# The first units of a two-block transformer kernel and its mLSTM heads, put in another order

## The chip, the cores and the metric

The kernel runs on one core of a Trainium2 chip. The metric is the device time of one execution in microseconds (us); below, a median of three runs. A core has a matrix engine (TensorE, PE in the profile; its weight loads are PEld), a vector engine (VectorE, DVE), a scalar engine (ScalarE, ACT), a general engine (GpSimd, POOL) and a queue engine (SyncE, SP). Each works through its own instruction list in order. An instruction waits on semaphores that others raise.

## The reference

The reference computes two transformer blocks in fp32 over 512 tokens of width 1024. Only the start of the first matters here:

```python
h = rmsnorm(x, norm_mix_g)
proj = h @ w_in                     # q_m, k_m, v_m, if_pre, o_pre, q_a, k_a, v_a, gate_pre
qk = silu(causal_depthwise_conv(concat([q_m, k_m]), conv_w, conv_b))
if_pre = if_pre + b_gate_if
ig, lf = if_pre[..., :4], log_sigmoid(if_pre[..., 4:])
hm = mlstm_cell(q_m, k_m, v_m, ig, lf)          # 4 heads of 256
hm = (hm - mean(hm)) * rsqrt(var(hm) + EPS) * mlstm_norm_g
y_a = sigmoid(o_pre) * hm
...                                 # windowed attention, merge, FFN; then a GLA + NSA block
```

`log_sigmoid` is computed as min(f, 0) - ln(1 + exp(-|f|)). The mLSTM cell is computed for all 512 tokens at once, in 128-token blocks: scores k·q, weights exp(...)·scores, numerators and divisor from weights·v.

## The kernel before

**Units.** All dense products are cut into units: one 1024 x 128 block of weights (512 KB) by the activations, 128 x 512 out. `UNITS` lists them in order: unit 0 and 1 are `qm` 0 and 1, unit 2 is `if` (the gates), unit 3 `vm` 0, units 4 and 5 `km` 0 and 1, unit 6 `vm` 1. Before the change unit 7 is `qm` 2 and unit 8 the output gate `om` 0. For accuracy a weight w is split into hi + lo (`WH`, `WL`), and so are the activations (`HH`, `HL`); each of a unit's eight k-blocks takes three matmuls (L947 to L949), so a unit takes 24.

**Who does what for a unit.** SP loads its weights into one of three `RAW` buffers (L886) when the split of three units earlier has read them. ACT makes `WH` (L1310), which also needs the unit of three earlier to be multiplied. The rest, `WL`, is made by DVE (L1576) or, for some odd units, by POOL (L2188). PE multiplies into a PSUM bank, and DVE evicts it, multiplied by the norm's factor `RB` (L1610).

**The start.** For each of eight k-blocks of x, ACT makes `HH` (L1296) and a square for the norm (L1302), DVE makes `HL` (L1561), and POOL adds the squares up (L2179) in an accumulator; the squares turn through two buffers. The norm's sum goes through PE (`fold`, L961), DVE (L1581) and POOL (a power, L2193) back to PE (`spread`, L987), and ACT copies the result to `RB` (L1318). Nothing can be evicted before `RB` is there. `lead` runs units 0 and 1 side by side, two k-blocks of each in turn, then unit 2.

**After the eviction.** A `qm` or `km` unit goes through a convolution on DVE (L1720 and three of L1724), a tanh on ACT (L1370) and a product on DVE (L1737). The gates take a chain of small 4 x 512 operations on DVE, then exp and ln on ACT (`gates_1`, L1379 and L1382), DVE again (`gates_2`, L1795 to L1804), and an exp (L1387). A `vm` unit, once evicted, is transposed on PE (L1012).

**Order.** One program is walked by each engine in turn; it fixes each engine's list. `quarter` and `unit` issue a unit's products with `flush` between, and `flush` issues the next step of each evicted unit (first tanh, then the product). `ahead(e, i)` issues the split of unit i + 2 and the load of unit i + 5. So the place of an `ahead`, an `evict` or a `flush` in the program sets its place in the lists of ACT and DVE. Here unit 1's tanh comes out of the `flush` inside unit 2, its product out of that inside unit 3; the gates' steps are issued in between.

**The heads.** After the gates' columns are turned (L1030), each head's scores (L1047), numerators (L1060) and transposes of hm (L1069) are spread over eight units' quarters by `Fill`.

Of the kernel before, what the change touches and what calls it, by code (L numbers as in the profile page):

```python
# [28 lines left out]
for _name, _n in [("ident", 128), ("big", 128), ("mean", 128), ("sel", 512), ("ba", 512), ("bc", 124),  # L29
                  ("m01", 124), ("glam", 128), ("unfold", 128), ("strip", 4),  # L30
                  ("residue", 4)]:
    CON[_name] = _at
    _at += _n
# [13 lines left out]
def unit_order():  # L47
# [27 lines left out]
    head(0, {1: ("if", 0, 0, 8)})  # L75
    for h in range(3):
        head(h + 1, {0: ("om", 2 * h, 0, 8), 3: ("om", 2 * h + 1, 0, 8)})
# [41 lines left out]
OB = 7  # L119

NSA_PARTS = [(0, (0, 1)), (3, (0,)), (3, (1,)), (2, (0,)), (2, (1,)), (1, (0, 1))]

# [40 lines left out]
class Order:  # L163
# [16 lines left out]
    def turn_bank(self, *key):  # L180
        self.hold(5 + self.turn % 2, *key)
# [7 lines left out]
    spread_max = scores = numerators = last_norm = gated = split_ya = none  # L189
# [163 lines left out]

def mlstm(e):
    lead(e, 0, "n1", False)
# [11 lines left out]
    e.store_vectors()  # L367
    e.turn_bank("columns")
    e.gate_columns()
    e.ring = [0, 1]  # L370
    at = 7
    for h in range(4):
        n = 8 if h < 3 else 11
        fill = Fill(e, range(at, at + n), 15)
        at += n
        e.turn_bank("max", h)
        e.spread_max(h)
        fill()
        for s in range(4):
            e.hold(SB[s % 3], "scores", h, s)  # L380
            e.scores(h, s)
            fill()
        for t in range(4):
            e.hold((OB, *SB)[t], "numer", h, t)
            e.numerators(h, t)
            fill()
        e.last_norm(h)
        fill(4)
        for j in range(2):
            e.turn_bank("hm", h, j)  # L390
        e.gated(h)
        fill()
        e.split_ya(h)
        fill()
        fill.drain(h == 3)
# [245 lines left out]
def build(nc, xT_d, wst_d, con_d, col_d, relb_d, oh_d, wa2_d, w1_d, w2_d, out_d, scr_d):  # L641
# [6 lines left out]
    with ExitStack() as ctx:  # L648
# [44 lines left out]
        con_in, col_in, table_in, vector_out = (signal(n, 16) for n in ("con_in", "col_in", "table_in", "vector_out"))  # L693
# [12 lines left out]
        def con(name, a=0, b=None, p0=0, p1=128):  # L706
            n = {"ident": 128, "big": 128, "mean": 128, "sel": 512, "ba": 512, "bc": 124, "m01": 124, "glam": 128,
# [28 lines left out]
        def spread_column(x, n=128):  # L736
# [5 lines left out]
        (hq0, hq1, hk0, hk1, hv0, hv1, so, xc, yc, th_, Mb, Md, E0, E1, WT, hm, yf_m, acol, ecol, stat, r0, r1, r2,  # L742
         r3) = parts(4608, 1024, 1024, 1024, 1024, 1028, 1028, 1024, 516, 512, 512, 512, 128, 512, 512, 1280, 1024, 512,
# [1666 lines left out]
```

## Time and profile before

| | |
|---|---|
| median of 3 runs | 2049.53 us (2048.44 to 2050.86) |
| profiled execution | 2049.81 us, span 2048.0 us |
| PE busy | 1971.6 us, 96% of the span |
| DVE busy | 1053.1 us, 51% |
| ACT busy | 635.0 us, 31% |
| POOL busy | 285.9 us, 14% |
| chain that ended last | PE 86%, DVE 9%, ACT 3% |
| granted TensorE clock, mean | 0.981 |

The span runs from the first instruction to the last. The chain that ended last is followed back from the end: a stretch of it on an engine is time in which nothing else could have helped. PE is nearly always busy, so what matters is the few stretches in which it stands still, and those in which the clock granted to it is half of full speed.

### The profile page before, as it was taken

To read this page: it belongs to the slowest core of one execution; us is meant where nothing else is said; L and a number is where in the kernel's file an instruction comes from. 1 tells how busy PE (TensorE), PEld (TensorE's weight loads), DVE (VectorE), ACT (ScalarE), POOL (GpSimd) and SP (SyncE) were. 2 spreads that over 40 slices of the span, in tenths; PEclk is the share of its full clock that TensorE was granted. 3 is DMA by queue.
4 is the path that set the end of the run, shared out by engine and by line. 5 is a ranking of instruction groups with operands and counts; after the bars stand their busy time and mean duration, and the time that the engine had idled before them with its cause. 6 is when DMAs were issued, how large, how long until landed. Compare 5 with 4: busy or idle time off the path is not lost.

```text
span 2048.0 us, 23700 instructions
## 1 busy us (share of the span) xinstructions
PE 1971.6 (96%) x9642; PEld 1596.9 (78%) x9642; DVE 1053.1 (51%) x1507; ACT 635.0 (31%) x1053; POOL 285.9 (14%) x190
## 2 busy tenths in 40 slices
PE   6999999999999999999998988999999999999997
PEld 5777788888888888888886777777777878888885
DVE  6666644344555644344344655546676644344344
ACT  4333322223333432222233322224344333222221
POOL 3122220011111111010021000111111131011012
PEclk9999999999999999999998899999999999999998
DMA  4222223232211323232322211221110322323322
GB/s 158 65 82 72 83 83 113 92 94 72 83 62 49 118 93 102 93 102 94 97 79 76 72 52 62 83 93 63 56 62 34 118 62 93 103 93 98 98 83 71
DMA packets 52444, 171.87 MB, mean 84 GB/s; under 512 B 5879, under 2 KB 9279, under 8 KB 52336
## 3 DMA queue, kind: packets, MB, share of 16 engines
q1 hardware_dynamic: 51616, 169.21, 25.9%
q8 instruction: 77, 1.26, 0.3%
q10 hardware_dynamic: 720, 1.15, 0.2%
q14 instruction: 31, 0.25, 0.0%
HBM read 168.12 MB, written 2.21 MB: 83 GB/s over the span
## 4 chain that ended last, share of the span: by engine, by line
PE 86%; DVE 9%; ACT 3%; issue 1%; POOL 1%; DMA 0%; DVEq 0%; POOLq 0%; ACTq 0%
PE PS L947 26%; PE PS L949 25%; PE PS L948 25%; PE PS L1245 1%; DVE WL L1576 1%; PE PS L1060 1%; PE PS L1047 1%; PE PS L1223 1%; PE PS L1267 1%; PE PS L1012 1%; PE PS L1084 1%; PE PS L1093 1%; PE PS L1107 1%; ACT WH L1310 1%; DVE AR L1610 1%
## 5 line engine op out<-in xcount | busy, mean ns | idle before, releaser
L947 PE MATMUL PS<-HH,WH 128*128 128x512 f32 x1368 | 549.3, 402 | 15.5 <-DVE WL L1576 12.2
L949 PE MATMUL PS<-HH,WL 128*128 128x512 f32 x1368 | 536.6, 392 | 0.0
L948 PE MATMUL PS<-HL,WH 128*128 128x512 f32 x1368 | 535.7, 392 | 0.0
L947 PE MATMUL PS<-AH,WH 128*128 128x512 f32 x1096 | 438.6, 400 | 11.5 <-DVE WL L1576 5.3
L1576 DVE TENSOR_TENSOR WL<-RAW,WH 128x1024 fp32r<-128x1024 f32 (+2 forms) x257 | 325.1, 1265 | 218.0 <-ACT WH L1310 216.3
L1310 ACT ACTIVATE WH<-RAW 128x1024 fp32r<-128x1024 f32 (+2 forms) x320 | 325.7, 1018 | 357.1 <-PE PS L949 357.0
L949 PE MATMUL PS<-AH,WL 128*128 128x512 f32 x1096 | 431.7, 394 | 0.0
L948 PE MATMUL PS<-AL,WH 128*128 128x512 f32 x1096 | 431.6, 394 | 0.0
L947 PEld LDWEIGHTS PS<-HH,WH 128*128 128x128 f32 x1368 | 258.8, 189 | 76.2 <-DVE WL L1576 10.9
L949 PEld LDWEIGHTS PS<-HH,WL 128*128 128x128 f32 x1368 | 258.5, 189 | 55.6
L948 PEld LDWEIGHTS PS<-HL,WH 128*128 128x128 f32 x1368 | 259.0, 189 | 53.5 <-issue 1.0
L947 PEld LDWEIGHTS PS<-AH,WH 128*128 128x128 f32 x1096 | 209.3, 191 | 59.2 <-issue 9.8
L2188 POOL TENSOR_TENSOR WL<-RAW,WH 128x1024 fp32r<-128x1024 f32 (+1 forms) x63 | 143.7, 2282 | 777.3 <-ACT WH L1310 777.3
L949 PEld LDWEIGHTS PS<-AH,WL 128*128 128x128 f32 x1096 | 208.8, 190 | 45.2
L948 PEld LDWEIGHTS PS<-AL,WH 128*128 128x128 f32 x1096 | 209.6, 191 | 42.4
L1610 DVE TENSOR_TENSOR AR<-PS,RB 128x512 f32<-128x512 f32 (+2 forms) x141 | 101.4, 719 | 212.7 <-PE PS L949 205.7
L2213 POOL TENSOR_TENSOR AR<-AR,RB 128x512 f32<-128x512 f32 x44 | 56.9, 1294 | 573.8 <-ACT AR L1348 573.8
L1348 ACT ACTIVATE AR<-AR 128x512 f32<-128x512 f32 x44 | 27.8, 632 | 159.1 <-DVE AR L1610 159.1
L2179 POOL TENSOR_TENSOR AR<-AR 128x512 f32<-128x512 f32 x36 | 48.2, 1346 | 144.0 <-ACT AR L1302 143.6
L1660 DVE TENSOR_TENSOR AR<-AR,PS 128x512 f32<-128x512 f32 x44 | 30.2, 687 | 71.1 <-PE PS L949 65.7
L1502 ACT ACTIVATE AR<-AR 128x128 f32<-128x128 f32 (+3 forms) x64 | 35.4, 554 | 93.1 <-DVE AR L2080 93.1
L1429 ACT ACTIVATE AR<-AR 128x256 f32<-128x256 f32 (+1 forms) x64 | 30.9, 485 | 87.8 <-DVE AR L1879 87.8
(241 smaller groups left out, 1432.1 us busy)
## 6 DMA issues: line engine op xcount, KB each, us to landing
RAW<-wst SPq DMA_DIRECT2D x288, 512.0 KB, 3.4
RAW<-wst SPq DMA_DIRECT2D x16, 384.0 KB, 3.0
RAW<-wst SPq DMA_DIRECT2D x16, 256.0 KB, 2.5
XT<-xT SPq DMA_DIRECT2D x3, 512.0 KB, 7.9
AR<-scr SPq DMA_DIRECT2D x16, 64.0 KB, 4.3
AR<-scr SPq DMA_DIRECT2D x8, 128.0 KB, 4.7
AR<-w SPq DMA_DIRECT2D x2, 512.0 KB, 4.1
out<-XT SPq DMA_DIRECT2D x4, 256.0 KB, 2.0
```

Of the source, the lines that this page charges most:

```text
L947: T.matmul(out, wh, XH[:, k, :], start=k == 0, stop=False)
L948: T.matmul(out, wh, XL[:, k, :], start=False, stop=False)
L949: m = T.matmul(out, wl, XH[:, k, :], start=False, stop=k == nk - 1)
L1310: t = A.activation(WH[:, i % NW, 0:n], RAW[:, i % NR, 0:n], ACT.Copy, scale=1.0)
L1429: t = A.activation(P, P, ACT.Exp, bias=ST[hp % 2][:, x, 0, b, i:i + 1], accum_out=ST[hp % 2][:, x, 1, b, i:i + 1])
L1502: t = A.activation(P, P, ACT.Exp, bias=NST[x][:, 0, hd, m:m + 1], accum_out=NST[x][:, 1, hd, m:m + 1])
L1576: t = V.tensor_tensor(WL[:, i % NW, 0:n], RAW[:, i % NR, 0:n], f(WH[:, i % NW, 0:n]), ALU.subtract)
L1610: return V.tensor_tensor(dst, src, rb, ALU.mult)
L1660: V.tensor_tensor(p, ffn_tile(name, j, 1), src, ALU.mult).then_inc(*bank_read.next(*free))
L2179: t = G.tensor_tensor(acc, acc, sums(norm, n), ALU.add)
L2188: t = G.tensor_tensor(WL[:, i % NW, 0:n], RAW[:, i % NR, 0:n], f(WH[:, i % NW, 0:n]), ALU.subtract)
L2213: t = G.tensor_tensor(ffn_tile(name, j, 1), ffn_tile(name, j, 0), RB, ALU.mult)
```

## The change

Six things, in the order of the program.

1. At the start ACT loads its function table on a dummy element before it waits for anything; it splits the weights of units 0 and 1 before the squares of those blocks; unit 1's `WL` goes from POOL to DVE, unit 2's from DVE to POOL (`lo_on_pool`). x is loaded whole before unit 2's weights.
2. The squares get eight buffers, so that none waits for POOL's additions.
3. The constants come in two transfers: the first 129 columns (identity and mean) on ACT's queue, the rest on SP's after unit 4's weights.
4. `lead_first` takes the place of `lead` for the first three units: `fold` comes after all of units 0 and 1 and a quarter of unit 2, `spread` two quarters later, and unit 4's split is issued behind `spread` instead of ahead of it.
5. `om` 0 and 1 become units 7 and 8, before the first head; the gates' columns are turned after them.
6. In each head the four scores stand together, with the transposes of the head before; the weights are made in place of the exponentials, the four numerators stand together, and the four divisors are one operation each over four columns. The matmuls are the same. The turn banks are 6 and 7 instead of 5 and 6, the fourth numerator's 5 instead of 7.

```diff
     head(0, {1: ("if", 0, 0, 8)})
+    add("om", 0)
+    add("om", 1)
     for h in range(3):
-        head(h + 1, {0: ("om", 2 * h, 0, 8), 3: ("om", 2 * h + 1, 0, 8)})
+        head(h + 1, {0: ("om", 2 * h, 0, 8), 3: ("om", 2 * h + 1, 0, 8)} if h else {})
...
+def lo_on_pool(i):
+
+    return i == 2 or (i % 2 == 1 and i > 1 and UNITS[i][0] in BUSY_DVE)
...
+def lead_first(e):
+
+    for i in range(3):
+        e.sum_bank("sum", i)
+    ahead(e, 0)
+    for k in range(0, 8, 2):
+        e.products(0, range(k, k + 2))
+        e.products(1, range(k, k + 2))
+    e.products(2, range(0, 2))
+    e.turn_bank("fold", "n1")
+    e.fold("n1")
+    ahead(e, 1)
+    e.products(2, range(2, 6))
+    e.turn_bank("spread", "n1")
+    e.spread("n1")
+    ahead(e, 2)
+    evict(e, 0)
+    flush_all(e)
+    evict(e, 1)
+    e.products(2, range(6, 8))
+
+
 def mlstm(e):
-    lead(e, 0, "n1", False)
+    lead_first(e)
     e.ones()
     quarter(e, 3, 0)
     e.gates_1()
...
     e.store_vectors()
+    unit(e, 7)
+    unit(e, 8)
     e.turn_bank("columns")
     e.gate_columns()
     e.ring = [0, 1]
-    at = 7
+    at = 9
     for h in range(4):
-        n = 8 if h < 3 else 11
-        fill = Fill(e, range(at, at + n), 15)
+        n = (6, 8, 8, 11)[h]
+        fill = Fill(e, range(at, at + n), 1)
         at += n
+        mlstm_scores(e, h)
+        fill.quarters(4)
+        e.weights(h)
+        fill.quarters(12 if h else 8)
+        for t in range(4):
+            e.hold((*SB, OB)[t], "numer", h, t)
+        e.numerators(h)
+        fill.quarters(6)
+        e.normed(h)
...
+def mlstm_scores(e, h):
+
+    if h < 4:
         e.turn_bank("max", h)
         e.spread_max(h)
...
+    if h:
+        e.turn_bank("hm", h - 1, 0)
+        e.gated(h - 1, 0)
+    if h < 4:
+        for x in range(3):
+            e.hold(SB[x], "scores", h, x)
+        e.scores(h, (0,))
+    if h:
+        e.turn_bank("hm", h - 1, 1)
+        e.gated(h - 1, 1)
+    if h < 4:
+        e.scores(h, (1, 2, 3))
+    flush(e)
+    if h:
+        e.split_ya(h - 1)
...
                     d.then_inc(*x_in[g].next("x", g))
-                    if g < 3:
+                    if g < 2:
                         s.load(g)
-                S.dma_start(C[:, :], con_d).then_inc(*con_in.next("con"))
+                s.load(2)
...
                 s.load(3)
                 s.load(4)
+                n = CON["big"]
+                S.dma_start(C[:, n:NCON], con_d[:, n:NCON]).then_inc(*con_rest_in.next("con_rest"))
...
                 A.dma_start(COL[:, :], col_d).then_inc(*col_in.next("col"))
+                A.dma_start(C[:, 0:CON["big"]], con_d[:, 0:CON["big"]]).then_inc(*con_in.next("con"))
+                act.wait_ge(*at("awake"))
+                A.activation(RC[:, 13:14], RC[:, 12:13], ACT.Copy, scale=1.0)
                 act.wait_ge(*at("col"))
-                for j in range(8):
-                    act.wait_ge(*at("x", (0, 1, 2, 2, 3, 3, 4, 4)[j]))
-                    s.scaled_hi("h1", HH, j, XT[:, j, :], col("mix_g", j))
-                    s.square("n1", j, XT[:, j, :])
-                    if j in (1, 3):
-                        s.split(j // 2)
-                act.wait_ge(*at("con"))
+                for js in ((0,), (1,), (2, 3), (4, 5, 6, 7)):
+                    for j in js:
+                        act.wait_ge(*at("x", (0, 1, 2, 2, 3, 3, 4, 4)[j]))
+                        s.scaled_hi("h1", HH, j, XT[:, j, :], col("mix_g", j))
+                    if js[0] < 2:
+                        s.split(js[0])
+                    for j in js:
+                        s.square("n1", j, XT[:, j, :])
```

Three places show how the lists move. On ACT, around the gates, before (L1310 is a unit's hi split, L1318 the copy to `RB`, L1370 the tanh of a `qm` or `km` unit, L1379 the gates' exp, L1382 their ln, L1387 their second exp):

```order
L1310 ACTIVATE WH<-RAW 128x1024 [waits unit_sum,raw_in1]
L1318 ACTIVATE RB<-PS 128x512 [waits pe_norm]
L1370 ACTIVATE AR<-AR 128x512 [waits dve_mlstm] x2
L1310 ACTIVATE WH<-RAW 128x1024 [waits unit_sum,raw_in2]
L1379 ACTIVATE AR<-AR 4x512 [waits dve_mlstm]
L1382 ACT_TABLE_LOAD
L1382 ACTIVATE AR<-AR,COL 4x512 [waits act_mlstm]
L1387 ACT_TABLE_LOAD
L1387 ACTIVATE AR<-AR 4x512 [waits dve_mlstm]
```

The same place after the change (L1375 the hi split, L1383 the copy to `RB`, L1435 the tanh, L1444 exp, L1447 ln, L1452 the second exp):

```order
L1383 ACTIVATE RB<-PS 128x512 [waits pe_norm]
L1375 ACTIVATE WH<-RAW 128x1024 [waits unit_sum,raw_in1]
L1435 ACTIVATE AR<-AR 128x512 [waits dve_mlstm]
L1375 ACTIVATE WH<-RAW 128x1024 [waits unit_sum,raw_in2]
L1444 ACTIVATE AR<-AR 4x512 [waits dve_mlstm]
L1447 ACT_TABLE_LOAD
L1447 ACTIVATE AR<-AR,COL 4x512 [waits act_mlstm]
L1435 ACT_TABLE_LOAD
L1435 ACTIVATE AR<-AR 128x512
L1452 ACTIVATE AR<-AR 4x512 [waits dve_mlstm]
```

The copy to `RB` now stands ahead of unit 4's hi split. Of the two tanh operations the second, unit 1's, has moved behind exp and ln, and the second table load stands before it.

On DVE, from unit 4's `WL` to the eviction of unit 3, after the change (L1647 is `WL`, L1681 an eviction, L1791 and L1795 the convolution, L1808 the product behind a tanh, L1859 the last step that the gates' exp waits for). Before, the list is the same in this stretch, but for a wait on ACT's ln that comes behind it:

```order
L1652 TENSOR_SCALAR RC<-PS 128x4 [waits pe_norm]
L1647 TENSOR_TENSOR WL<-RAW,WH 128x1024 [waits weight_hi,raw_in1]
L1681 TENSOR_TENSOR AR<-PS,RB 128x512 [waits act_norm,unit_sum]
...
L1859 SCALAR_TENSOR_TENSOR AR<-AR 4x512 [waits dve_mlstm]
L1861 MEMSET AR 4x512
L1808 SCALAR_TENSOR_TENSOR AR<-AR 128x512 [waits act_mlstm]
L1681 TENSOR_TENSOR AR<-PS,RB 128x512 [waits unit_sum]
```

Unit 4's `WL` stands ahead of the first eviction, and unit 1's product ahead of unit 3's eviction, in both lists; what has moved is on ACT.

## Rows read from the trace of the kernel before

**Rows 1.** Busy time by stretch: each engine's busy us, PEclk, DMA share, GB/s.
```profile
50.00:56.00 6.00, 6.00 (x17) 4.50 (x18) 4.46 (x5) 2.62 (x4) 0.00 (x0) 0.57 0.00 0
72.00:76.00 4.00, 4.00 (x14) 3.09 (x14) 0.00 (x0) 0.68 (x1) 2.37 (x1) 0.57 0.26 101
76.00:310.00 234.00, 234.00 (x1041) 187.98 (x1041) 139.67 (x273) 70.10 (x109) 46.65 (x32) 1.00 0.25 78
```

**Rows 2.** What PE waited for in 0 to 420 us: total, times, longest.
```profile
PE PS L947 <- DVE WL L1576: 10.9, 1, 10.9
PE PS L1012 <- DVE AR L1610: 6.9, 2, 5.7
PE PS L947 <- POOL WL L2188: 2.7, 1, 2.7
```

**Rows 3.** Readers of x, 0 to 60 us: ns min/median/max of one, starts.
```profile
L1296 ACT ACTIVATE HH<-XT,COL x8: 705/706/722, 5.9 to 18.7; 128x512 fp32r<-128x512 f32 x8
L1302 ACT ACTIVATE AR<-XT x8: 612/612/630, 6.5 to 19.8; 128x512 f32<-128x512 f32 x8
L1561 DVE SCALAR_TENSOR_TENSOR HL<-XT,COL,HH x8: 752/1770/2830, 6.7 to 20.3; 128x512 fp32r<-128x512 f32 x8
```

**Rows 4.** Users of the raw weights, 0 to 60 us.
```profile
L1310 ACT ACTIVATE WH<-RAW x8: 1039/1042/1061, 8.2 to 57.2; 128x1024 fp32r<-128x1024 f32 x8
L1576 DVE TENSOR_TENSOR WL<-RAW,WH x4: 1210/1360/2143, 9.3 to 57.1; 128x1024 fp32r<-128x1024 f32 x4
L2188 POOL TENSOR_TENSOR WL<-RAW,WH x4: 2403/2473/2803, 13.6 to 58.4; 128x1024 fp32r<-128x1024 f32 x4
DMA to landing us min/median/max: 3.4/4.0/7.4
```

**Rows 5.** POOL's additions, the same view of the arena tile.
```profile
L2179 POOL TENSOR_TENSOR AR<-AR x6: 1311/1548/1734, 8.4 to 19.9; 128x512 f32<-128x512 f32 x6
```

**Rows 6.** Timeline, the start and the lead: start us, us, instruction, idle before.
```profile
4.61 1.28 ACT L1296 ACT_TABLE_LOAD   x1 [4.61 <-DMA XT<-xT]
...
25.02 1.84 PE L961 MATMUL PS<-C,AR 128*128 128x1 f32 x16
...
32.30 1.05 PE L987 MATMUL PS<-C,RC 128*128 128x128 f32 x8
...
33.39 0.60 ACT L1318 ACTIVATE RB<-PS 128x512 f32<-128x512 f32 x1 [2.49 <-PE PS L987]
```

**Rows 7.** Timeline of DVE from the first eviction to unit 3's.
```profile
34.09 0.69 DVE L1610 TENSOR_TENSOR AR<-PS,RB 128x512 f32<-128x512 f32 x1 [0.95 <-ACT RB L1318]
...
44.76 2.55 DVE L1785 TENSOR_SCALAR AR<-AR,COL 4x512 f32<-4x512 f32 x1
...
48.50 0.61 DVE L1737 SCALAR_TENSOR_TENSOR AR<-AR 128x512 f32<-128x512 f32 x1
49.14 0.69 DVE L1610 TENSOR_TENSOR AR<-PS,RB 128x512 f32<-128x512 f32 x1
```

**Rows 8.** Timeline of ACT around the gates.
```profile
42.77 0.63 ACT L1370 ACTIVATE AR<-AR 128x512 f32<-128x512 f32 x1 [4.30 <-DVE AR L1774]
...
48.06 0.63 ACT L1379 ACTIVATE AR<-AR 4x512 f32<-4x512 f32 x1 [3.71 <-DVE AR L1788]
48.71 1.28 ACT L1382 ACT_TABLE_LOAD   x1
50.00 0.72 ACT L1382 ACTIVATE AR<-AR,COL 4x512 f32<-4x512 f32 x1
50.74 1.28 ACT L1387 ACT_TABLE_LOAD   x1
```

**Rows 9.** Timeline of PE at the stall before unit 3's transposes.
```profile
43.66 0.39 PE L948 MATMUL PS<-HL,WH 128*128 128x512 f32 x1
43.88 0.39 PE L949 MATMUL PS<-HH,WL 128*128 128x512 f32 x1
49.98 1.08 PE L1012 MATMUL PS<-C,AR 128*128 128x128 f32 x4 [5.71 <-DVE AR L1610]
```

## What the change was forecast to do, before its result was seen

> **What bounds the kernel now.** I read the busy time by stretch first. From 76 to 310 us, through all four heads, PE is busy for 234.00 of 234.00 us at granted clock 1.00 [rows 1]. The matmuls of this stretch are the same after the change, so it has nothing to give; it can only lose. What can move lies in the first 76 us. The list of what PE waited for gives three stalls there: 10.9 us until the first split weights, 2.7 us for POOL's `WL` of unit 1, 5.7 us at the transposes of unit 3 (L1012; the row's other wait, 1.2 us, comes at the entrance to attention, where the program is unchanged) [rows 2]. Two stretches run at half clock: in 50 to 56 us, after the long stall, and in 72 to 76 us, after the short matmuls of the gates' columns, the clock is 0.57, so they lose 6 x 0.43 = 2.6 and 4 x 0.43 = 1.7 us [rows 1].
>
> Then I asked what ends the third stall. PE has finished its matmuls at 44.3 and starts the transposes at 49.98 [rows 9]. It waits for DVE's eviction of unit 3 (49.14), and DVE has been in an unbroken chain since its first eviction at 34.09: two convolutions and the gates' small steps [rows 7]. That one began when ACT had written `RB`, at 33.39 + 0.60 = 33.99 [rows 6]. So all that happens on PE before 44 us is off the path unless it brings `RB` earlier. The end is set by: `RB`, what DVE does ahead of its first eviction, the chain to unit 3's eviction, the transposes.
>
> **When RB comes after the change.** The table load (1.28 us) now runs before x lands at 4.61 [rows 6]. ACT then makes `HH` 0 (0.71) and can split unit 0. Its weights are the second transfer in SP's list and land 3.4 to 7.4 us after their issue, median 4.0; before, ACT reached that split at 8.2, without a wait [rows 4]. I take 6.0 (bounds 5.3, when `HH` 0 is done, and 8.2). Split 1.04, DVE's rest 1.21 to 1.49 (the 2.14 is one beside POOL) [rows 4]: first matmul at 8.5 instead of 10.9.
>
> PE can't run ahead from there, since it needs `HL`. `HL` takes 0.75 us alone and 1.77 at the median [rows 3], because in this stretch a DVE operation with two SBUF inputs alternates with POOL's additions. The Trainium skill, "SBUF — State Buffer", Who interferes with whom, says that such an instruction and a GpSimd instruction that reads SBUF hold a shared port pair exclusively, the other blocked for the whole instruction; the trace agrees in the 0.75 against 1.77 us. By it the eight buffers don't help DVE, since they only let POOL queue its additions sooner. `HH` 2 is done at 6.0 + 1.04 + 0.61 + 0.71 + 1.04 + 0.61 + 0.71 = 10.7 [rows 3, 4]. Six `HL` at 1.77 end at 21.3 (at 0.75 throughout: 15.2). Behind the last one stand nine matmuls. One starts every 0.228 us: 43.66 and 43.88 are two neighbours [rows 9], and 24 take 5.46 us. So units 0 and 1 end at 21.3 + 2.0 = 23.3. Unit 2's `WL` is on POOL behind six additions; the last three can't begin before square 4 at about 16.0, 3 x 1.55 and then 2.4 to 2.8 end at 23.2 [rows 4, 5]. Both paths meet at 23.3; a later one alone would cost. The `HL` path alone could save 6 us, the POOL path can't: with additions of 1.31 it ends at 22.3. So 23.3 has little room below, 1 us, and more above.
>
> From there to `RB`: 18 matmuls of unit 2 (4.1), fold 1.8, spread 1.0, ACT 0.6 [rows 6]: 30.8. That is 3.2 us before the old 33.99.
>
> **Ahead of the first eviction.** Unit 4's hi split now stands behind the copy to `RB` on ACT, and its rest ahead of the eviction on DVE. Before, both were done while PE was still in `spread`. Now they cost 1.04 + 1.2 (alone) to 2.1 (beside POOL) [rows 4]; I take 1.2 and 0.1 of hand-over. First eviction at 33.1, against 34.09: of the 3.2 us, 1.0 is left.
>
> **The chain.** From 34.09 to the start of the gates' exp at 48.06 it is 13.97 us [rows 7, 8]. One step of it, 2.55 us for a 4 x 512 operation where the wider product beside it takes 0.61 [rows 7], was held by POOL's `WL` of unit 5. After the change unit 5's split comes earlier, beside unit 1's convolution, whose steps have SBUF inputs too: I leave the 1.9 us in (bounds: 1.9 less, or another 0.9, up to a POOL split of 2.8 [rows 4]). Exp starts at 47.1.
>
> Here the change adds a wait. Unit 1's tanh was issued before the gates and was done at 43.4 [rows 8]. Now it stands behind exp and ln, and ln uses another table. On ACT: exp to the second table load took 50.74 - 48.06 = 2.68, then the load 1.28 and the tanh 0.63 [rows 8], together 4.6: tanh is done at 51.7. Behind it on DVE wait unit 1's product, then unit 3's eviction, and PE's transposes behind that; from product to transposes it was 49.98 - 48.50 = 1.48 [rows 7, 9]. **PE resumes at 53.2 instead of 49.98: 3.2 us later.** The stall itself grows from 5.7 to some 13.5 us: PE, done with units 0 and 1 at 23.3, has 60 matmuls (13.7), fold and spread (2.8) until it arrives, at 39.8.
>
> Whether a table switch costs more than its row is the second rule weighed. Rows first: the load ends at 49.99 and ln starts at 50.00 [rows 8]. The Trainium skill, "ScalarE: Activation LUTs", What ACT_TABLE_LOAD costs, puts a drain of about 1.38 us beside the load, some 2.66 us for a switch. By it the two switches would cost 2.8 us more, and the sum would be 2054.1 us. The rows leave no room for it.
>
> **After the stall.** The gates' second half waits for ln no longer (DVE did, before, after unit 3's eviction), so nothing behind is later relative to PE. Half clock after resuming: 2.6 us in both [rows 1]; a stall is above the length that already halved the clock. Turning the columns and the max now stand together with 4.3 us of full-width fp32 scores behind them, and the third short matmul (the bias vector) is moved two units ahead of them. Of the 1.7 us lost in 72 to 76 [rows 1] I take all as regained; the other end is nothing.
>
> **The heads.** Md, divisors and norms are fewer and wider operations; DVE was busy 140 of 234 us [rows 1], and PE waits for none of it. The tight place is head 1's scores: unit 13's convolution and product must be done one unit plus about 1.5 us after its matmuls. By my count 1.3 us is to spare, and one clash with POOL (up to 2.4 us [rows 4]) would cost up to 1.1. Bounds 0 and 1.1; I take 0. The second part of the constants lands some 50 us before its first use, the first part lies beside the x transfers, bank numbers cost nothing.
>
> **The sum.** Own time of the profiled execution 2049.8 (0.3 above the median of the runs, and it is what I add to): + 3.2 - 1.7 = **2051.3 us**.
>
> **The rivals.**
> - *The second half-clock stretch stays.* For it: columns and max are still short matmuls in a row, some 1.6 us. Against: they were longer, and full-width work now stands on both sides. 2053.0 us.
> - *The tanh isn't last.* If ACT's switch were hidden, PE would resume at 33.1 + 15.9 = 49.0: - 1.0 - 1.7 gives 2047.1. For it: `RB` is earlier. Against: ACT and DVE take their lists in order, and the load stands right before that tanh. With POOL's clash gone as well, 1.9 less: 2045.2, faster.
> - *The cold start: slower.* PE gets its work in groups of 3 and 9 matmuls, as `HL` arrives. If it is granted half clock (0.43 us each, twice the pitch) until unit 2, units 0 and 1 take 48 x 0.43 = 20.6 from 8.5, to 29.1 instead of 23.3, and `RB` and everything behind move with it, since the path runs through `RB`: up to + 5.8, 2057.1. It decides the sign at 2.3 us, ten matmuls or so. Half the effect is 2054.2. The same place gives 1 to 2 us if x or unit 1's weights land late.
> - *The drain of the skill's page:* 2054.1, as above.
>
> **The numbers.** 0.2%, 4.1 us, is about what a measurement of this kernel can tell from no change: 2045.4 to 2053.6 counts as the same. Forecast 0.44 (own range 2049.5 to 2053); second stretch stays 0.22; tanh not last 0.11, of which 0.05 faster; cold start or late weights 0.20, of which 0.02 stay below the bound; drain 0.03. Faster 0.06, same 0.73, slower 0.21. Range 2046.5 to 2055.5: it leaves out the deep end of the cold start and the case of everything early.
>
> **What would show it.** Right: PE's first matmul near 8.5; `RB` near 31; the first eviction behind a `WL` of DVE at about 33; on ACT load, ln, load, tanh in one row; PE's wait at L1067 of 12 to 14 us, ended by DVE's eviction at 53. Wrong: this wait ending before 50.5 (then the table switch isn't on the path), `RB` after 33 (then the start is colder than taken), or any PE wait over 1 us between 80 and 310 us (then the heads have a price).

## The result, and the profile after

The changed kernel took 2054.1 us (median of 12 runs, 2049.74 to 2055.49), the kernel before on the same chip 2049.18 (12 runs, 2045.55 to 2051.50): a ratio of 1.0022, 95% interval 1.0013 to 1.0031. A second comparison, in the experiments below, gave 1.0016 [1.0007, 1.0025] (2054.17 against 2050.4 us). The forecast was 2051.3 with a range of 2046.5 to 2055.5. So the time lies in the range, but 2.8 us above the forecast, and just past the 2053.6 us at which the prediction began its slower case (chance 0.21). One of tanh_first's twelve runs below took 2229.59 us at a granted clock of 0.84; its ratio leaves that run out, and without it the median is 2050.38 instead of 2050.64 us.

The profiled execution took 2053.67 us, span 2051.9, against 2049.81 and 2048.0 before. Busy time by stretch first, with PEclk as the third number from the end, the answer to [rows 1]:

```profile
50.00:56.00 6.00, 3.40 (x11) 2.89 (x12) 4.82 (x6) 1.00 (x2) 0.00 (x0) 0.51 0.00 0
72.00:76.00 4.00, 4.00 (x21) 3.28 (x21) 1.04 (x2) 0.56 (x1) 2.39 (x1) 1.00 0.52 163
76.00:310.00 234.00, 233.42 (x1045) 187.73 (x1044) 138.66 (x226) 69.75 (x110) 44.15 (x24) 1.00 0.25 79
```

The second half-clock stretch is gone (1.00 in 72 to 76 us), and PE is busy for 233.42 of 234 us in the heads, against 234.00. What PE waited for in 0 to 310 us, against [rows 2]:

```profile
PE PS L1067 <- DVE AR L1681: 13.2, 1, 13.2
PE PS L1002 <- DVE WL L1647: 8.2, 1, 8.2
PE PS L1002 <- DVE HL L1632: 1.0, 3, 0.4
PE PS L1107 <- DVE AR L1808: 0.6, 1, 0.6
```

The long stall is 13.2 us (forecast 13.5), the first matmul starts at 8.25 (8.5), and head 1's scores wait 0.6 us (0, bound 1.1). The readers of x and POOL's additions, against [rows 3, 5]:

```profile
L1632 DVE SCALAR_TENSOR_TENSOR HL<-XT,COL,HH x8: 744/1776/1780, 5.3 to 18.7; 128x512 fp32r<-128x512 f32 x8
L2252 POOL TENSOR_TENSOR AR<-AR x6: 1550/1558/1807, 9.6 to 18.4; 128x512 f32<-128x512 f32 x6
```

`HL` still takes 1.78 us at the median. The first eight matmuls of PE start 0.43 us apart (8.84, 9.27, 9.69 and so on to 11.40), later ones 0.23, and PE then waits for `HL`. The timeline from the fold to the first eviction, against [rows 6, 7]:

```profile
24.29 1.84 PE L1016 MATMUL PS<-C,AR 128*128 128x1 f32 x16
...
29.91 0.60 ACT L1383 ACTIVATE RB<-PS 128x512 f32<-128x512 f32 x1 [7.25 <-PE PS L1042]
30.40 1.05 ACT L1375 ACTIVATE WH<-RAW 128x1024 fp32r<-128x1024 f32 x1
31.55 1.23 DVE L1647 TENSOR_TENSOR WL<-RAW,WH 128x1024 fp32r<-128x1024 f32 x1 [5.23 <-ACT WH L1375]
32.70 0.68 DVE L1681 TENSOR_TENSOR AR<-PS,RB 128x512 f32<-128x512 f32 x1
```

`RB` is written at 30.5, 3.5 us ahead of before, and unit 4's split takes 2.1 of them back: the first eviction is at 32.70, 1.4 us ahead of before. Then the gates, against [rows 7 to 9], all engines:

```profile
46.41 0.63 ACT L1444 ACTIVATE AR<-AR 4x512 f32<-4x512 f32 x1 [8.39 <-DVE AR L1859]
46.43 0.48 DVE L1861 MEMSET AR<- 4x512 f32 x1
47.06 1.28 ACT L1447 ACT_TABLE_LOAD   x1
48.35 0.72 ACT L1447 ACTIVATE AR<-AR,COL 4x512 f32<-4x512 f32 x1
49.09 1.28 ACT L1435 ACT_TABLE_LOAD   x1
50.38 0.63 ACT L1435 ACTIVATE AR<-AR 128x512 f32<-128x512 f32 x1
51.05 0.69 DVE L1808 SCALAR_TENSOR_TENSOR AR<-AR 128x512 f32<-128x512 f32 x1 [4.13 <-ACT AR L1435]
51.77 0.69 DVE L1681 TENSOR_TENSOR AR<-PS,RB 128x512 f32<-128x512 f32 x1
52.38 0.67 DVE L1866 SCALAR_TENSOR_TENSOR AR<-AR 4x512 f32<-4x512 f32 x1
52.60 1.08 PE L1067 MATMUL PS<-C,AR 128*128 128x128 f32 x4 [13.18 <-DVE AR L1681]
```

Load, ln, load, tanh stand in one row, then product, eviction, transposes: PE resumes at 52.60 (forecast 53.2, before 49.98). Up to here all is as forecast. But where the 4 us are is shown by the first transposes of the attention part (L1012 before, L1067 after), at the end of all that the change touches. Before and after:

```profile
312.01 0.63 PE L1012 MATMUL PS<-C,AR 128*128 128x128 f32 x4 [1.24 <-DVE AR L1610]
```

```profile
311.73 0.63 PE L1067 MATMUL PS<-C,AR 128*128 128x128 f32 x4 [1.24 <-DVE AR L1681]
```

The changed kernel is 0.3 us **ahead** there. It stays 0.3 to 0.4 ahead until 1092 us, and from 1202 us to the end it is 3.7 to 4.0 behind. So the loss lies in 1092 to 1200 us, the start of the GLA part, whose instructions stand in the same order in both kernels. Busy time by stretch there, before:

```profile
1116.00:1122.00 6.00, 5.01 (x23) 3.65 (x24) 2.28 (x5) 1.91 (x2) 0.00 (x0) 1.00 0.00 1
1122.00:1132.00 10.00, 10.00 (x27) 6.16 (x26) 5.55 (x9) 6.14 (x9) 0.00 (x0) 0.66 0.01 2
1142.00:1148.00 6.00, 4.65 (x21) 3.55 (x20) 3.95 (x6) 1.88 (x3) 0.00 (x0) 1.00 0.14 40
1148.00:1152.00 4.00, 4.00 (x19) 3.32 (x18) 2.61 (x4) 2.40 (x4) 0.00 (x0) 1.00 0.25 92
```

And after:

```profile
1116.00:1122.00 6.00, 4.60 (x16) 3.79 (x17) 1.54 (x3) 1.91 (x2) 0.00 (x0) 0.72 0.03 10
1122.00:1132.00 10.00, 10.00 (x41) 6.56 (x40) 6.70 (x10) 4.26 (x6) 0.00 (x0) 1.00 0.00 0
1142.00:1148.00 6.00, 1.45 (x7) 0.90 (x7) 4.06 (x7) 2.40 (x4) 0.00 (x0) 1.00 0.00 0
1148.00:1152.00 4.00, 4.00 (x11) 3.14 (x12) 2.29 (x4) 2.42 (x3) 0.00 (x0) 0.57 0.44 131
```

In the changed kernel a half-clock piece falls at 1117 to 1121 us, in the kernel before at 1123 to 1130 us. During the first, VectorE waits for what PE makes: its copy of a unit's transposes (L1768 before, L1839 after) starts at 1120.85 us before and at 1122.73 us after, and only 0.4 of these 1.9 us were there when PE took up its work at 1117 us. Before and after:

```profile
1120.85 0.69 DVE L1768 COPY AR<-PS 128x512 f32<-128x512 f32 x1 [2.45 <-PE PS L1012]
```

```profile
1122.73 0.69 DVE L1839 COPY AR<-PS 128x512 f32<-128x512 f32 x1 [3.73 <-PE PS L1067]
```

The second piece lies where PE is ahead of the engines that feed it, so the lost time comes out of a later wait. In the changed kernel PE has full clock there and arrives early: its stall for VectorE's `WL` is 4.55 us instead of 1.35, and the clock halves once more behind it (1148 to 1151 us). Going by the starts of the same VectorE operations, the changed kernel loses 0.8 us between 1092 and 1101 us (where half clock lasts 6.8 us instead of 3.4), 1.5 between 1110 and 1121, 1.6 between 1146 and 1160 and 0.3 behind that. The stall in the kernel before and in the changed one:

```profile
1146.01 0.47 PE L947 MATMUL PS<-AH,WH 128*128 128x512 f32 x1 [1.35 <-DVE WL L1576]
```

```profile
1147.88 0.58 PE L1002 MATMUL PS<-AH,WH 128*128 128x512 f32 x1 [4.55 <-DVE WL L1647]
```

### The profile page after: what moved, and what is told of

Its sections match the earlier page's. It is cut to its first block, busy times and chain, and to the rows that moved or that the text cites. A ratio compares the mean times of both kernels' runs of the same rounds, so it can differ in the third digit from the quotient of the medians.

```text
span 2051.9 us, 23633 instructions
## 1 busy us (share of the span) xinstructions
PE 1968.4 (96%) x9642; PEld 1595.8 (78%) x9642; DVE 1050.4 (51%) x1460; ACT 633.9 (31%) x1054; POOL 283.5 (14%) x182
## 4 chain that ended last, share of the span: by engine, by line
PE 85%; DVE 9%; ACT 3%; issue 1%; POOL 0%; DMA 0%; DVEq 0%; SPq 0%
PE PS L1002 25%; PE PS L1003 25%; PE PS L1004 25%; DVE WL L1647 1%; PE PS L1306 1%; PE PS L1107 1%; PE PS L1122 1%; PE PS L1284 1%; PE PS L1328 1%; PE PS L1067 1%; ACT WH L1375 1%; PE PS L1145 1%; DVE AR L1681 1%; PE PS L1154 1%; PE PS L1168 1%
## 5 line engine op out<-in xcount | busy, mean ns | idle before, releaser
L1002 PE MATMUL PS<-HH,WH 128*128 128x512 f32 x1368 | 541.7, 396 | 11.3 <-DVE WL L1647 9.5
L1375 ACT ACTIVATE WH<-RAW 128x1024 fp32r<-128x1024 f32 (+2 forms) x320 | 325.8, 1018 | 366.6 <-PE PS L1004 365.8
L1647 DVE TENSOR_TENSOR WL<-RAW,WH 128x1024 fp32r<-128x1024 f32 (+2 forms) x257 | 323.8, 1260 | 217.6 <-ACT WH L1375 215.8
L1681 DVE TENSOR_TENSOR AR<-PS,RB 128x512 f32<-128x512 f32 (+2 forms) x141 | 101.4, 719 | 235.9 <-PE PS L1004 229.8
```

What stands on the lines that cost most here:

```text
L1002: T.matmul(out, wh, XH[:, k, :], start=k == 0, stop=False)
L1375: t = A.activation(WH[:, i % NW, 0:n], RAW[:, i % NR, 0:n], ACT.Copy, scale=1.0)
L1647: t = V.tensor_tensor(WL[:, i % NW, 0:n], RAW[:, i % NR, 0:n], f(WH[:, i % NW, 0:n]), ALU.subtract)
L1681: return V.tensor_tensor(dst, src, rb, ALU.mult)
```

## The experiments

Two questions: are the 4 us fixed in the changed program (theory S), or do they hang on where half clock falls (theory C)? And do the steps of the forecast stand in the price that it gave them? "Entrance" is the start of those first transposes, "at 1202" the start of the VectorE operation that the kernel before starts at 1201.99 us; both, like "PE resumes" (after the stall), in the one profiled execution. A shift is against the first profile of before. The medians come from five comparisons; the kernel before took 2049.18 us beside changed, 2050.4 beside after_again, tanh_first, split4_first and both_first, 2048.76 beside the two `gla_filled`, stall_filled and gates_between, 2049.05 beside old_lead, three_squares and before_again, and 2049.07 beside best.

| kernel | PE resumes | entrance (shift) | at 1202, shift | profiled, us | median, us |
|---|---|---|---|---|---|
| before | 49.98 | 312.01 | 0 | 2049.81 | 2049.18 |
| before_again | 50.06 | 311.94 (-0.1) | -2.45 | 2049.37 | 2049.19 |
| changed | 52.60 | 311.73 (-0.3) | +3.72 | 2053.67 | 2054.10 |
| after_again | 52.67 | 311.61 (-0.4) | +0.20 | 2049.91 | 2054.17 |
| tanh_first | 48.73 | 308.76 (-3.2) | +0.02 | 2051.55 | 2050.64 |
| split4_first | 50.52 | 310.81 (-1.2) | -1.06 | 2050.45 | 2053.03 |
| both_first | 46.79 | 307.20 (-4.8) | -6.33 | 2043.76 | 2046.25 |
| old_lead | 46.69 | 305.66 (-6.3) | -5.70 | 2044.01 | 2046.12 |
| three_squares | 52.54 | 312.94 (+0.9) | -0.58 | 2049.49 | 2052.59 |
| gates_between | 52.68 | 313.11 (+1.1) | +5.13 | 2055.06 | 2053.84 |
| stall_filled | 52.69 | 311.90 (-0.1) | +0.13 | 2051.74 | 2052.39 |
| before_gla_filled | 50.48 | 312.14 (+0.1) | -4.06 | 2046.14 | 2047.65 |
| after_gla_filled | 52.78 | 312.05 (0.0) | -2.74 | 2047.32 | 2047.74 |
| best | 46.50 | 305.36 (-6.7) | -7.72 | 2042.31 | 2040.18 |

**after_again**: the changed kernel, unchanged.

> The changed kernel once more, to see what of its time repeats. In the first profile its mLSTM part ended 0.3 us ahead of the kernel before (transposes at the entrance to attention 311.73 against 312.01 us), and the 4 us were lost between 1101 and 1194 us, in code that both have alike. Theory C (clock): which stretches there get half clock hangs on where the chip's grants fall, so this profile has fold (L1016, 1101 us) at the same time within 0.3 us, but the stretch from there to 1194 us takes another length than 92.8 us in at least some profiles (before: 89.2). Theory S (systematic): the stretch repeats at 92.8 within 0.5 us, and the total at 2053 to 2055 us.

Its profiled execution took 2049.91 us, 3.8 less than the first one, with the same program and the same entrance. The same stretches as above:

```profile
1116.00:1122.00 6.00, 4.83 (x23) 3.63 (x24) 2.32 (x5) 1.91 (x2) 0.00 (x0) 1.00 0.01 2
1122.00:1132.00 10.00, 10.00 (x28) 6.23 (x27) 5.69 (x9) 6.00 (x9) 0.00 (x0) 0.66 0.01 2
1142.00:1148.00 6.00, 4.64 (x21) 3.55 (x20) 4.08 (x6) 1.75 (x3) 0.00 (x0) 1.00 0.12 24
```

From 1100 us on it reads as the kernel before. Theory S falls for the single execution: one program shows both courses. But the two don't come equally often. Of the 24 runs of the changed kernel 20 took over 2052 us and 4 took 2049.7 to 2050.0, with nothing between; of the 118 runs of the kernel before in the five comparisons 9 took over 2052. That the runs above 2052 are those of the long course is read from the two profiled ones (2053.67 and 2049.91 us); the others have no trace.

**before_again**: the kernel before, unchanged.

> The kernel before once more, for its trace. Theory C: up to the entrance to attention it repeats within 0.2 us (312.0), and from 1092 us on it may take another path, up to 4 us either way, with the half-clock pieces elsewhere.

Entrance within 0.1 us, the same course to 1169 us, and then a half-clock piece that the first profile has is missing, behind the same 3.7 us of idle time. First profile, then this one:

```profile
1172.00:1176.00 4.00, 2.94 (x9) 2.57 (x10) 3.97 (x6) 0.00 (x0) 0.00 (x0) 0.50 0.18 43
```

```profile
1172.00:1176.00 4.00, 3.06 (x16) 2.62 (x17) 3.84 (x6) 0.00 (x0) 0.00 (x0) 1.00 0.23 61
```

That puts it 2.45 us ahead at 1202 us; pieces elsewhere take 2.0 of it back by the end. So within the kernel before, too, half clock falls differently from one execution to the next.

**before_gla_filled** and **after_gla_filled**: the same edit in each, which gives PE full-width work in two idle times of the GLA part.

```diff
                     if k == 0:
                         s.free("sum", i)
+                        if i == unit_of("small2") + 1:
+                            for _ in range(4):
+                                T.matmul(out, ident(), con("sel"), start=True, stop=True)
                         pe.wait_ge(*at("lo", i))
...
                 if name == "small2":
+                    for _ in range(2):
+                        T.matmul(PS[:, b, :], ident(), con("sel"), start=True, stop=True)
                     pe.wait_ge(*at("tanh", i))
```

> The kernel before, with six full-width matmuls whose result is thrown away: four in the 4 us stall ahead of the GLA part's second unit (PE idle 1088 to 1092 us) and two in the 2 us wait ahead of the small gates' transposes (1115 to 1117). Nothing computed changes. Theory C (clock): the half-clock piece at 1092 to 1096 us, some 2 us of loss, goes, the pieces behind it move, and the total falls to 2045 to 2049, with less spread than the 2045.7 to 2055.0 of the kernel as it is. Theory S (a fixed cost in the program): the matmuls are hidden or cost up to 5.5 us, total 2050 or more.

> The same six thrown-away matmuls in the changed kernel. Theory C: the 4 us between the two kernels come from where the half clock falls, not from the change's own region, which ends 0.3 to 0.4 us ahead at the entrance to attention; with the same filling the two kernels' profiles should differ by under 2 us at 1200 us, and their medians by less than the 4 us they differ as they are. Theory S: the changed kernel stays 4 us above the filled kernel before.

The medians are 2047.65 (0.9989 [0.9979, 0.9998] of before) and 2047.74 us (0.9995 [0.9987, 1.0004]). The 4.9 us between the two kernels (3.8 in the second comparison) have become 0.1 by the medians and 1.2 by the ratios, whose intervals overlap, and their ranges, 2045.5 to 2049.1 and 2046.3 to 2049.9, no longer hold a group above 2052. At 1202 us the two profiles are 1.3 us apart. The filled matmuls of the kernel before and the first one behind them, then the stretch in three kernels, before, before_gla_filled, after_gla_filled (an fp32 matmul stands as two in the rows, so four are x8):

```profile
1088.13 3.59 PE L947 MATMUL PS<-C 128*128 128x512 f32 x8
1092.22 0.50 PE L950 MATMUL PS<-AH,WH 128*128 128x512 f32 x1 [0.50 <-DVE WL L1581]
```

```profile
1084.00:1098.00 14.00, 8.79 (x31) 6.51 (x30) 8.60 (x9) 5.91 (x9) 3.96 (x4) 0.88 0.29 90
```

```profile
1084.00:1098.00 14.00, 12.24 (x46) 8.18 (x45) 8.61 (x9) 6.01 (x9) 4.04 (x4) 1.00 0.27 90
```

```profile
1084.00:1098.00 14.00, 12.28 (x46) 8.25 (x45) 8.60 (x9) 5.85 (x9) 3.87 (x4) 1.00 0.28 90
```

The filled work displaces none of the real (PE takes up unit `small2` + 1 at 1092.22 in both the kernel before and the filled one), and the clock is 1.00 in this stretch. This is the experiment that shows the cause by taking it away: the half clock of 1090 to 1097 us is gone from both kernels (the changed one has none now until 1138 us), the change does not touch this part, and the difference in the median is gone with it, as far as the intervals tell.

**tanh_first**: unit 1's tanh before the gates.

```diff
     evict(e, 1)
+    flush(e)
     e.products(2, range(6, 8))
```

> Only unit 1's tanh is issued before the gates again, as it was before. My prediction's step says: the load, ln, load chain on ScalarE leaves the path. After the gates' last VectorE step at 45.7 + 0.6 come unit 1's product (0.69), unit 3's eviction (0.69) and the transposes: PE resumes at 47.8 instead of 52.6, 4.8 us earlier, and the attention entrance moves from 311.7 to about 307. Theory L (local): the total falls by as much, to about 2049. Theory C (clock): the entrance moves by 4.8, but the total by 4.8 plus or minus up to 4, as the stretch 1085 to 1194 us falls out otherwise. Rival (the tanh isn't what PE waited for): PE resumes at 52 or later, total 2054.

PE resumes at 48.73 us, 3.9 us earlier, not 4.8.

With the tanh moved, ScalarE's split of unit 5 comes behind it, POOL's `WL` of unit 5 begins at 43.24 instead of 38.16, and it lies beside a 4 x 512 operation of the gates, which takes 2.55 us instead of 0.47; in the changed kernel it lay beside unit 1's first convolution step (2.38 instead of 0.55). So the clash of [rows 7] only changes its victim, as the forecast left it in; and a memset of 0.5 us ahead of the product was forgotten in the 4.8. That the tanh is on the path of what PE waits for last is shown. Of the 3.2 us by which the entrance is ahead of the kernel before, none are left at 1202 us.

**split4_first**: unit 4's split where it was.

```diff
+    ahead(e, 2)
     e.turn_bank("spread", "n1")
     e.spread("n1")
-    ahead(e, 2)
     evict(e, 0)
```

> Only unit 4's split is moved ahead of the spread, where it was before; the tanh stays behind the gates. My prediction took 2.2 us for it: ScalarE's 1.05 and VectorE's 1.2 stand between the copy to RB and the first eviction. Expected: RB copy unchanged at 29.9, first eviction at 30.5 instead of 32.7, all of the chain 2.1 us earlier, PE resumes at 50.5 instead of 52.6, entrance to attention at 309.6. Theory L: total 2.1 lower, about 2052. Theory C: total anywhere from 2048 to 2056 with the entrance at 309.6. Rival: VectorE is held by POOL instead, and the eviction gains under 1 us.

PE resumes at 50.52, 2.1 us earlier, where the forecast's term was 2.3 (1.04 + 1.2 + 0.1). Only 0.9 of it reaches the entrance, since the half clock after the stall lasts to 56 us, as late as in the changed kernel, and the median moved by 1.1.

**both_first**: both edits.

> Both edits together: unit 4's split ahead of the spread and unit 1's tanh before the gates. If both stand in one chain, PE resumes at 45.7 instead of 52.6 (4.8 + 2.1 earlier), the stall is 6.3 us, the entrance to attention at 304.9 and by theory L the total at about 2047, below the kernel before. Theory C: entrance as said, total 2043 to 2051. Rival: something else is last once the tanh is gone (PE's own work ends at 39.4), and the sum of the two is under 5 us.

PE resumes at 46.79 (3.9 + 2.1 would be 46.6), the entrance is at 307.20 and the median 2046.25, ratio 0.9982 [0.9973, 0.9991]: below both kernels. The two terms add up in one chain.

**old_lead**: the first three units in their old order, the rest of the change kept.

```diff
 def mlstm(e):
-    lead_first(e)
+    lead(e, 0, "n1", False)
```

> The changed kernel with the order of the first three units as it was: fold ahead of the last quarter of units 0 and 1, spread after half of unit 2, units 2 to 4 split one step earlier, unit 1's tanh ahead of the gates; the rest of the change (weights ahead of squares, eight buffers, constants in two transfers, gates' move, heads) stays. From the traces: PE waits for HL in 10 to 20 us, so a fold of 1.7 us there is partly hidden, and six matmuls fewer (1.4 us) stand ahead of the spread. Expected by these rows: RB at 28.6 (30.5 in the changed kernel), PE resumes at 45 against 46.8 with both edits of the earlier run, entrance to attention at 305 to 306. Rival: the fold there waits for POOL's last addition (20.5 us) and PE loses up to 2 us, RB near 30.5 and the entrance at 307. Totals: theory C says anything from 2 below to 4 above what the entrance gives, 2041 to 2049.

Half right. `RB` comes at 30.7, not 28.6: the fold at 20.09 waited 0.6 us for POOL and took 1.92, and a half-clock piece fell behind it. The two rows are of this kernel, around the fold and after the stall:

```profile
22.00:26.00 4.00, 4.00 (x12) 3.13 (x12) 0.16 (x1) 1.06 (x1) 1.98 (x3) 0.57 0.39 131
46.00:52.00 6.00, 5.31 (x18) 3.82 (x18) 4.94 (x6) 2.71 (x3) 0.00 (x0) 0.72 0.10 39
```

PE resumes at 46.69, as in both_first, yet the entrance is 1.5 us earlier, because the half clock after the stall ends earlier (by 50 against 53 us). So the new place of fold and spread gains 0.2 us at `RB` (30.7 against 30.5) and nothing that the time shows; median 2046.12, 0.9982 [0.9973, 0.9990], is both_first's.

**three_squares**: the first norm's squares in three buffers.

```diff
-        SUMS = {"n1": parts(13836, *[512] * 8), "n2": [SS0[:, 0:512], SS0[:, 512:1024], SS1[:, 0:512]],
+        SUMS = {"n1": parts(13836, *[512] * 3), "n2": [SS0[:, 0:512], SS0[:, 512:1024], SS1[:, 0:512]],
...
-            if name == "n1":
-                return SUMS[name][n]
...
-                if n > 2 and norm != "n1":
+                if n > 2:
                     act.wait_ge(*at("acc", norm, n - 2))
```

> The changed kernel with the squares of the first norm in three buffers as before (ScalarE's square waits for POOL's addition two before it), all else as changed. My prediction: the eight buffers don't help VectorE, they only let POOL queue its additions sooner. Expected: HL still about 1.7 us each, fold, spread and RB within 0.5 us of 24.45, 28.98 and 29.91, entrance at 311.7 within 0.5. Rival: ScalarE's waits push HH 4 to 7 and unit 2's split back, RB 1 to 3 us later, entrance up to 314.7. Total not told apart below 2 us.

`RB`'s copy starts at 29.85 and PE resumes at 52.54, both 0.06 us from the changed kernel, and `HL` takes 1.78 us at the median as there: the eight buffers do nothing for VectorE or the path. The entrance is 1.2 us later all the same, as half clock lasted to 58.5 us instead of 55.8. Row of three_squares:

```profile
52.00:60.00 8.00, 7.46 (x21) 5.20 (x22) 6.15 (x8) 2.07 (x4) 0.00 (x0) 0.59 0.00 1
```

and of the changed kernel:

```profile
52.00:60.00 8.00, 7.40 (x26) 5.44 (x27) 6.15 (x8) 2.90 (x4) 0.00 (x0) 0.76 0.00 0
```

**gates_between**: the first two output gates back between head 1's units.

```diff
-    add("om", 0)
-    add("om", 1)
...
-    unit(e, 7)
-    unit(e, 8)
...
```

> The changed kernel with the first two output gates back between head 1's units, where they were; the gates' columns and head 0's scores follow unit 6. My prediction's step: the half-clock piece at 72 to 76 us (1.7 us) went because full-width work stands on both sides of the short matmuls. Expected if the gates' move did that: a half-clock piece comes back within 5 us after the columns, and the entrance to attention moves from 311.7 to 313.4. Rival: the new heads (wide scores behind the columns) did it, clock 1.00 there and entrance within 0.3 us of 311.7, or later by a wait of head 0's scores for unit 6's convolution.

The half-clock piece is back, and the entrance 1.4 us later than the changed kernel's:

```profile
72.00:76.00 4.00, 4.00 (x13) 1.74 (x12) 1.74 (x5) 1.90 (x5) 0.00 (x0) 0.79 0.53 163
76.00:80.00 4.00, 4.00 (x18) 2.87 (x17) 0.00 (x0) 2.43 (x6) 1.43 (x1) 0.79 0.00 0
```

It costs 8 x 0.21 = 1.7 us. The half clock after the stall also lasts longer than in the changed kernel (to 57.2 instead of 55.8 us, 0.7 us lost), and the two together are 1.0 us more than the 1.4 at the entrance: with the gates back, PE's wait of 0.6 us at head 1's scores is gone too, and 0.4 us stay unexplained. So the gates' new place, and not the new heads, keeps the clock up there in these profiles, and about 1 us of the 1.7 that they save is lost again in the heads.

**stall_filled**: twelve thrown-away matmuls in the 13.2 us stall.

```diff
                     src, dst = unit_tokens(i)
+                    if i == 3:
+                        pe.wait_ge(*at("con_rest"))
+                        for _ in range(12):
+                            T.matmul(PS[:, b, :], ident(), con("sel"), start=True, stop=True)
                     pe.wait_ge(*at("free", "sum", i))
```

> The changed kernel with twelve full-width matmuls whose result is thrown away in PE's 13.2 us stall ahead of unit 3's transposes (39.4 to 52.6 us); at about 0.95 us each they end near 50.8. Theory: the half clock of 52.6 to 55.9 us comes from the idle time ahead of it; PE still resumes at 52.6, the clock stays at 1.00, and the entrance to attention is 1.6 us earlier, at 310.1. Rival: the half clock comes from the short transposes themselves or stays whatever PE did, entrance 311.7. The total may move by 1.6 plus or minus 4 with the GLA part's grants.

The expected 310.1 did not come: they took 0.87 us each, not 0.95, and left 2.8 us idle. The first row is of the transposes, the second of busy time in 53 to 58 us:

```profile
52.69 0.66 PE L1071 MATMUL PS<-C,AR 128*128 128x128 f32 x4 [2.80 <-DVE AR L1685]
```

```profile
53.00:58.00 5.00, 5.00 (x18) 3.37 (x15) 4.00 (x5) 0.83 (x2) 0.00 (x0) 0.66 0.00 0
```

The clock was full at the transposes (0.66 us against 1.08) and halved at 54.0 us, 1.3 us after they began. The half clock lost 1.7 us, as much as behind the 13.2 us in the changed kernel (1.6).

**best**: both edits, seven matmuls in the stall (1.0 us left idle), six in the GLA part.

> The changed kernel with both edits (unit 4's split ahead of the spread, unit 1's tanh before the gates), seven thrown-away full-width matmuls in what is left of the stall ahead of unit 3's transposes (39.7 to 46.8 us; at 0.87 us each they end at 45.8, so PE idles 1.0 us at the end), and the six of the GLA part. From the runs before: with both edits the entrance to attention is at 307.2 (4.8 ahead of the kernel before), and if under 1 us of idle time keeps the clock at 1.00, the half clock after the stall goes too, 305.6 to 306. The filling took 1 us off the median of the kernel before and 6 off the changed one. Theory C: median 2042 to 2044, below every kernel so far, and little spread. Rival: the half clock comes after the filled stall as it did after the one filled up to 2.8 us (then 307, and 2044 to 2046).

2040.18 us (5 runs, 2039.15 to 2042.31), 0.9955 [0.9941, 0.9968] of before. Its transposes, and its busy time in 40 to 80 us:

```profile
46.50 0.66 PE L1077 MATMUL PS<-C,AR 128*128 128x128 f32 x4 [0.98 <-DVE AR L1691]
```

```profile
40.00:80.00 40.00, 38.01 (x151) 25.02 (x150) 28.22 (x38) 15.09 (x21) 7.33 (x3) 1.00 0.25 82
```

The clock is 1.00 throughout. With its median best is 9 us faster than the kernel before, and below the 2042 to 2044 expected.

## Why the prediction was right, and where it was wrong

- **Start of PE, `HL`, `RB`.** Right: 8.25 for 8.5; `HL` at 1.78 for 1.77; `RB` at 30.5 for 30.8. The cold start, a rival, came for the first eight matmuls only (0.43 us apart), and the 1.6 us were hidden: PE still had to wait 1.0 us for `HL` behind them. That `HL` is not helped by the buffers is shown by three_squares.
- **Ahead of the first eviction.** Right: 32.70 for 33.1; split4_first measures the term at 2.1 for 2.3.
- **The chain.** Right: 46.41 - 32.70 = 13.7 for 14.0, with the POOL clash left in at 1.8 us, on another operation.
- **The tanh behind the gates' table loads.** Right: 50.38 + 0.63 = 51.0 for 51.7, PE at 52.60 for 53.2. tanh_first shows it as the last wait. Its net price is 3.9 us, where the forecast had 4.2 (53.2 less 49.0). The rival of the drain falls, as the rows of the first load show: 47.06 + 1.28 = 48.34, ln at 48.35. So the changed kernel shows no gap either, against the drain of 1.38 us that is put beside the load by the Trainium skill, "ScalarE: Activation LUTs", What ACT_TABLE_LOAD costs.
- **Half clock after the stall, "2.6 us in both".** Wrong in size: 3.3 us at half clock in the changed kernel, 1.6 lost. It isn't a price of the stall: with PE resuming within 0.1 us, the end of the half clock was 55.8 us (changed) or 58.5 (three_squares). The error is 1 us and of chance sign.
- **The second half-clock stretch.** Right: gone, and gates_between brings it back at 1.7 us. But the same move has a price in the heads, about 1.0 us by gates_between, where the forecast took 0 (bound 1.1).
- **Heads at nothing.** 0.6 us of wait, inside the bounds; the mLSTM part as a whole came out at -0.3 against the forecast's +1.5, by the 1 us above, 0.6 of the earlier PE start after the stall, and small change.
- **The step that failed is the sum itself:** "own time of the profiled execution + 3.2 - 1.7". It carried the shift of the changed region to the end of the program unchanged. Between 1092 and 1202 us an unchanged program took 3.4 us more or less from one execution to the next, which is more than any term of the sum. The median moved because, as read above, the long course came in 20 of 24 runs instead of 9 of 118. That the number lies in the range is luck: the region that the sum priced came out at -0.3 us instead of +1.5, and the range was wide enough for the 4 us from elsewhere because of a cold start that cost nothing. It is chance, too, that 2054.1 is the figure of the rival of the drain, and nearly that of half a cold start: the trace shows no drain and no cost of the cold start. None of the prediction's signs of being wrong came: the stall ended at 52.6 us, `RB` at 30.5, and no wait of PE between 80 and 310 us was over 1 us.

What stays open is why the changed kernel meets the long course so much more often. The shift at the entrance doesn't order it. Take the median, less that of the kernel before in the same comparison, less the shift at the entrance: +5.2 and +4.2 us for the changed kernel in its two comparisons, +4.0 for gates_between (+1.1 us at the entrance), +3.8 for split4_first (-1.2), +3.7 for stall_filled (-0.1), +3.5 for tanh_first (-3.2), +3.4 for old_lead (-6.3), +2.6 for three_squares (+0.9), +0.7 for both_first (-4.8). All the versions of the changed kernel without filling in the GLA part lie above zero, and the three kernels with it at -1.1 to -2.2. The traces add one thing: the idle time of PE that ends near 1146 us (1136 to 1149) is 4.5 us in nine of the eleven traces of the changed kernel and its versions, and 1.4 us in the other two and in the three of the kernel before. In all nine a half-clock piece begins during it or within 0.8 us of its end, in none of the other five. That the kernel before just sits in a lucky place, and that something in the changed program beyond its timing matters, have not been told apart.

## What to carry to other kernels

The costs of the changed region alone don't decide the time here. Before a difference of 0.2% is put down to an edit, compare both traces at a landmark behind the edited region and again further on, and take a second profile of the same kernel. Where an engine's wait is replaced, look for a table load between the producer and the one that waits; issuing one tanh ahead of the gates let PE resume 3.9 us earlier. And where PE idles for a few microseconds ahead of work that is on the path, full-width matmuls into a bank that is about to be overwritten cost nothing here and, where they left 1.0 us idle or less, took out the half clock behind the stall; with 2.8 us left they did not.

## What the runs showed of the hardware

- The length of the idle time alone did not decide whether the clock fell to half (1.2 GHz). In the start of the GLA part, to 1270 us, half clock came with every idle time of 3.99 us and more in all the profiles; behind 3.7 us it was 0.50 in one profile of the kernel before and 1.00 in the other, behind 2.04 us both were seen in the changed kernel. In the filled stalls before unit 3's transposes, 2.8 us of rest ended in half clock and 0.98 did not. How long it lasted after the same stall of 13.2 us differed by 2.7 us (to 55.8 us in the changed kernel, to 58.5 in three_squares).
- A piece of half clock cost 1.5 us at 1117 to 1121 us (changed kernel, first profile) and nothing at 1123 to 1130 us (after_again), by whether the engines behind PE waited for it at that moment.
- An fp32 matmul of a 128 x 128 constant with 512 columns took 0.87 us (10.46 us for twelve), and the clock was 1.00 while the twelve ran, though their results were thrown away.
